# Two transformer blocks on one core: seven block products instead of eight in the feed-forward, expert strips loaded in pairs, unused products on TensorE

## What is computed

```python
def expert_choice_ffn(h, w_router, w_gate, w_up, w_down):   # 16 experts, 32 tokens each
    aff = softmax(h @ w_router)
    gates, idx = lax.top_k(aff.transpose(0, 2, 1), cap)
    xe = h[bidx, idx]
    a = einsum('becd,edf->becf', xe, w_gate)                # 1024 -> 2048
    b = einsum('becd,edf->becf', xe, w_up)
    ye = einsum('becf,efd->becd', silu(a) * b, w_down)      # 2048 -> 1024
    return zeros_like(h).at[bidx, idx].add(ye * gates)
...
x = x + g * rms_norm(p @ w_ple_proj, norm_ple_post)         # first block's end, "first projection"
...
kv = rmsnorm(mem, g_mem) @ w_mem_kv                         # second block's memory keys and values
...
h = rmsnorm(x, g_pre_ffn)                                   # second block's feed-forward
gate, up = split(h @ w_ffn_in)                              # 1024 -> 2 x 2816
x = x + rmsnorm((silu(gate) * up) @ w_ffn_down, g_post_ffn) # 2816 -> 1024
```

## Time and profile before

| | |
|---|---|
| median of 3 runs | 1776.91 us (1776.56 to 1779.11) |
| the profiled execution | 1774.88 us, its span 1773.1 us |
| TensorE busy | 1419.3 us, 80% |
| weight loads (beside it) | 769.1 us |
| VectorE, ScalarE, GpSimd busy | 324.1, 187.7, 34.6 us |
| DMA | 517.66 MB, mean 292 GB/s |
| granted clock | 0.91 |

### The profile page before, as it was taken

The page is one execution under the profiler, slowest core; times in us unless marked ns, Lnnn a source line. Parts: engine busy times, 40 slices in busy tenths (PEclk is TensorE's granted clock), DMA queues, the critical chain, the costliest instruction groups (busy, mean ns, idle before and its releaser), DMA issues.

```text
span 1773.1 us, 19596 instructions
## 1 busy us (share of the span) xinstructions
PE 1419.3 (80%) x7856; PEld 769.1 (43%) x7856; DVE 324.1 (18%) x798; ACT 187.7 (11%) x509; POOL 34.6 (2%) x96
## 2 busy tenths in 40 slices
PE   8978656766666567666666679999999999999998
PEld 5533111211121112111211126878777888677775
DVE  2442001200110011011001112345334101200001
ACT  2221000000000000000000001133223000100000
POOL 1100000000000000000000000000000000000000
PEclk9999888887887888878888879999999999999999
DMA  9668999999999999999999992123130336034431
GB/s 402 242 250 354 427 427 431 426 428 428 428 428 427 428 429 426 428 428 428 429 427 429 427 429 103 64 107 109 50 157 24 152 144 262 35 123 172 173 148 48
DMA packets 41112, 517.66 MB, mean 292 GB/s; under 512 B 4592, under 2 KB 5616, under 8 KB 8048
## 3 DMA queue, kind: packets, MB, share of 16 engines
q1 hardware_dynamic: 39152, 513.98, 69.4%
q10 hardware_dynamic: 1920, 3.11, 0.5%
HBM read 515.50 MB, written 1.05 MB: 291 GB/s over the span
## 4 chain that ended last, share of the span: by engine, by line
PE 53%; DMA 42%; DVE 2%; issue 1%; ACT 1%; SPq 0%; POOL 0%; ACTq 0%; POOLq 0%; PEldq 0%; DVEq 0%
PE ps L898 51%; DMA ring<-in_experts 42%; PE ps L1263 1%; PE ps L904 1%; DVE turned_T L1511 1%; ACT xn L770 0%; DVE scr L1623 0%; DMA vecs<-in_vecs 0%; PE ps L981 0%; ACT scr L776 0%; DVE xn L1747 0%; PE ps L957 0%; SPq L180 0%; PE ps L1357 0%; DVE scr L1591 0%
## 5 line engine op out<-in xcount | busy, mean ns | idle before, releaser
L898 PE MATMUL ps<-ring,scr 128*32 128x512 f32 (+1 forms) x3200 | 549.4, 744 | 260.7 <-DMA ring<-in_experts 245.5
L898 PEld LDWEIGHTS ps<-ring,scr 128*32 128x32 f32 (+1 forms) x3200 | 130.3, 128 | 638.8 <-DMA ring<-in_experts 400.3
L898 PE MATMUL ps<-turned_T,ring 128*128 128x256 f32 (+2 forms) x1984 | 384.4, 363 | 7.3 <-PE ps L898 3.1
L898 PEld LDWEIGHTS ps<-turned_T,ring 128*128 128x128 f32 (+1 forms) x1984 | 334.5, 186 | 57.9 <-issue 14.7
L898 PE MATMUL ps<-scr 128*128 128x512 f32 (+10 forms) x640 | 158.8, 406 | 19.5 <-DVE scr L1623 13.0
L898 PE MATMUL ps<-ring,turned_T 128*128 128x128 f32 (+3 forms) x640 | 170.8, 425 | 2.3 <-DVE turned_T L1511 1.5
L898 PEld LDWEIGHTS ps<-ring,turned_T 128*128 128x128 f32 x640 | 106.3, 190 | 64.4 <-issue 49.0
L898 PEld LDWEIGHTS ps<-scr 64*128 64x128 f32 (+4 forms) x640 | 83.2, 173 | 95.5 <-issue 51.4
L1626 DVE TENSOR_TENSOR x<-x,ps 128x512 f32<-128x512 f32 x64 | 44.0, 687 | 261.2 <-PE ps L898 261.2
L1618 DVE SCALAR_TENSOR_TENSOR scr<-scr,ps 128x512 f32<-128x512 f32 x16 | 11.0, 688 | 279.5 <-PE ps L898 279.5
L1616 DVE SCALAR_TENSOR_TENSOR scr<-scr,ps 128x512 f32<-128x512 f32 x16 | 11.0, 688 | 198.9 <-ACT scr L691 198.9
(11 more groups left out here) (243 smaller groups left out, 631.1 us busy)
## 6 DMA issues: line engine op xcount, KB each, us to landing
ring<-in_experts SPq DMA_DIRECT2D x188, 2048.0 KB, 24.6
ring<-in_w_ffn_in SPq DMA_DIRECT2D x11, 2048.0 KB, 9.1
ring<-in_w_merge SPq DMA_DIRECT2D x8, 1536.0 KB, 6.4
ring<-in_w_ffn_down SPq DMA_DIRECT2D x11, 1024.0 KB, 4.8
ring<-in_w_out SPq DMA_DIRECT2D x4, 2048.0 KB, 23.7
ring<-in_w_ml SPq DMA_DIRECT2D x4, 2048.0 KB, 7.8
ring<-in_w_nsa SPq DMA_DIRECT2D x4, 2048.0 KB, 7.7
ring<-in_w_proj SPq DMA_DIRECT2D x8, 1024.0 KB, 6.1
```

Of the source, the lines that this page charges most:

```text
L898: return pe.matmul(o, l, rr, start=start, stop=stop)
```

## The change

1. **Feed-forward.** Rows, columns and tokens are each cut in two, and seven products of blocks take the place of eight: sums of weight blocks, token blocks and results are made by VectorE. `ff_in` does it for each strip from step 1 on (step 0 stays), with 7 x 8 matmuls of 128 columns; step s's weight sums (`sums_in`) are made in step s-2. All 11 inputs' steps now come first, `hF` holds their results, and then `ff_down` pairs row block n with n + 11: seven matmuls of 512 columns for each of 11 strips, in seven banks. At the end VectorE puts the seven banks together (`total`) before ScalarE's squares and `post(1, 1.0)`. VectorE's `post` uses one buffer, now in `gains`.
2. **Expert strips.** From expert 2 on the first ten strips of an expert are loaded two at a time, 32 KB a partition in one DMA into two neighbouring slots (`load_two`), once both are free; the last two come singly. All groups use the same slots (`ROT`).
3. **First projection and memory weights.** They go to slot 9, no longer into the ring; the projection is issued after four strips of expert 1 and after expert 0's `h_sb`, each memory quarter after the first expert of its group.
4. **Products without use.** `idle` multiplies constants into bank 7: 6 products of 256 columns at the start, and 5, 22 and 4 of 128 columns in the router.

```diff
+HALF = D_FF // P // 2
+FF_SLOTS = [2, 4, 3, 5]
...
-ROTS = [3, 4, 5, 0]
-LAST_ROT = 1
-TAIL = [(n + LAST_ROT - 3) % SLOTS for n in range(SLOTS)]
+ROT = 2
+PAIRED = {0: (2, 2), 1: (2, 1), 2: (2, 2), 3: (2, 0), 4: (2, 2), 5: (2, 0)}
+TAIL = [(n + ROT - 3) % SLOTS for n in range(SLOTS)]
...
+    def load_two(self, slot, dst, src):
+        for s in (slot, slot + 1):
+            r = self.rounds[s]
+            self.eng.wait_ge(self.free[s], r)
+            if not isinstance(r, int):
+                self.eng.nop(nofuse=True)
+        self.eng.dma_start(dst, src).then_inc(self.full[slot], 16)
+        self.count(slot, 1)
+        self.count(slot + 1, 0)
...
-                    r.load(s, whole(s, "experts", e * 12 + n))
-            def experts(part, rot):
-                with sp.Fori(0, PARTS[part]) as i:
-                    r.enter(i, {s: (2, 2) for s in range(SLOTS)})
-                    expert(i + sum(PARTS[:part]), around(rot))
-                    r.leave(PARTS[part])
+                    r.load(s, strip_of(s, e, n))
+            def paired(e, slots):
+                for n in range(0, 10, 2):
+                    s = slots[n]
+                    r.load_two(s, ring[:, s * SLOT:(s + 2) * SLOT], packed["experts"][bass.ds((e * 6 + n // 2) * P, P), :])
+                for n in (10, 11):
+                    r.load(slots[n], strip_of(slots[n], e, n))
+            def experts(part, rot, first=0):
+                n = PARTS[part] - first
+                with sp.Fori(0, n) as i:
+                    r.enter(i, PAIRED)
+                    paired(i + sum(PARTS[:part]) + first, around(rot))
+                    r.leave(n)
+            def with_aside(part, quarter):
+                if quarter:
+                    paired(sum(PARTS[:part]), around(ROT))
+                    sp.wait_ge(mkv_ps, quarter)
+                else:
+                    for n, s in enumerate(around(ROT)):
+                        if n == 4:
+                            sp.wait_ge(h_sb, 1)
+                            sp.dma_start(*whole(9, "w_ple_proj", 0)).then_inc(full[9], 16)
+                        r.load(s, strip_of(s, 1, n))
+                    sp.wait_ge(e_ps, 4)
+                sp.dma_start(*whole(9, "w_mem_kv", quarter)).then_inc(full[9], 16)
+                experts(part, ROT, 1)
 
             expert(0, FIRST_SLOTS, FIRST_LOADS)
-            r.load(2, whole(2, "w_ple_proj", 0))
             for n in range(4):
-                experts(1 + n, ROTS[n])
-                r.load(ROTS[n], whole(ROTS[n], "w_mem_kv", n))
-            experts(5, LAST_ROT)
+                with_aside(1 + n, n)
+            experts(5, ROT)
...
+            for s in range(FF_STEPS):
+                r.load(FF_SLOTS[s % 4], whole(FF_SLOTS[s % 4], "w_ffn_in", s, tslot))
+            for n in range(HALF):
+                s = FF_SLOTS[(FF_STEPS + n) % 4]
+                r.load(s, whole(s, "w_ffn_down", n, tslot))
...
+            def idle(n, a):
+                for _ in range(n):
+                    mm(bank[7][:, 0:a.shape[1]], a[:, 0:P], a)
+            pe.wait_ge(idle_in, 1)
+            idle(6, sA[:, 0, 0, :])
...
+            idle(5, ident)
             pe.wait_ge(route_sb, 3)
...
+            idle(22, ident)
...
+                def arrived(s, n):
+                    if single or n % 2 == 0 or n == 11:
+                        r.arrived(s, 1)
+                    else:
+                        r.count(s, 0)
...
+            idle(4, ident)
             pe.wait_ge(sel_done, 2)
             pe.wait_ge(xn_done, 4)
-            expert(0, FIRST_SLOTS, selall[:, 0])
+            expert(0, FIRST_SLOTS, selall[:, 0], True)
...
-            r.arrived(2, 1)
-            wple = slot[2][:, 0:2 * D].rearrange("p (k n) -> p k n", k=2)
+            pe.wait_ge(full[9], 32)
+            wple = slot[9][:, 0:2 * D].rearrange("p (k n) -> p k n", k=2)
...
+            def ff_in(s, at):
+                par, b = at % 2, hT.rearrange("p (j k) (t n) -> p j t k n", j=2, t=NT)
+                w = tstrip[FF_SLOTS[at]].rearrange("p (j k) (i n) -> p j i k n", j=2, i=2)
+                sums = sF[1 - par]
+                half = lambda q: bank[4 - 4 * par + q // 2][:, (q % 2) * T:(q % 2 + 1) * T]
+                r.arrived(FF_SLOTS[at], 1)
+                if not isinstance(s, int) or s > 1:
+                    pe.wait_ge(ff_h, s * 2 - 2)
+                    pe.nop(nofuse=True)
+                for q, (l, rr) in enumerate(((w[:, 0, 0], b[:, 0, 0]), (w[:, 1, 0], b[:, 1, 0]),
+                                             (sums[:, 1], tT[:, 1]), (sums[:, 0], tT[:, 0]), (sums[:, 3], b[:, 1, 1]),
+                                             (sums[:, 2], tT[:, 2]), (w[:, 1, 1], tT[:, 3]))):
+                    if q == 2:
+                        pe.wait_ge(ff_sum, s + 1)
+                        pe.nop(nofuse=True)
+                    for f in range(2):
+                        for k in range(4):
+                            ins = mm(half(q)[:, f * P:(f + 1) * P], l[:, k, f * P:(f + 1) * P], rr[:, k, :], k == 0, k == 3)
+                            if (q, f, k) == (0, 0, 0):
+                                ins.then_inc(tfree[FF_SLOTS[(at - 1) % 4]], 1)
+                    if q in (1, 3, 5, 6):
+                        ins.then_inc(ff_ps, 1)
...
+            def ff_down(n):
+                s = FF_SLOTS[(FF_STEPS + n) % 4]
+                w = tslot[s][:, 0:2 * D].rearrange("p (j i n) -> p j i n", j=2, i=2)
+                a = [[hF[:, c // 2, t, c % 2, :] for c in (n, n + HALF)] for t in range(NT)]
...
+                for q, (l, rr) in enumerate(((a[0][0], w[:, 0, 0]), (a[0][1], w[:, 1, 0]), (ss[:, 1], tt[:, 1]),
+                                             (ss[:, 0], tt[:, 0]), (ss[:, 3], w[:, 1, 1]), (ss[:, 2], tt[:, 2]),
+                                             (a[1][1], tt[:, 3]))):
...
+                    ins = mm(bank[q], l, rr, n == 0, n == HALF - 1)
...
+            with pe.Fori(0, 2) as i:
+                r.enter(i, {s: (1, 1) for s in FF_SLOTS})
+                for n in range(2, 6):
+                    ff_in(i * 4 + n, n % 4)
+                r.leave(2)
+            ff_in(10, 2)
+            for n in range(HALF):
...
+            dve.memset(sA[:, 0, 0, :], 1.0).then_inc(idle_in, 1)
...
+            def sums_in(s, at):
+                par = at % 2
+                w = tstrip[FF_SLOTS[at]].rearrange("p (j k) (i n) -> p j i k n", j=2, i=2)
+                o = sF[1 - par]
+                dve.wait_ge(tfull[FF_SLOTS[at]], (s - at) * 4 + 16 + landed[FF_SLOTS[at]])
+                dve.nop(nofuse=True)
+                chain(dve.tensor_tensor(o[:, 0], w[:, 0, 1], w[:, 1, 1], ALU.add))
+                sub(o[:, 1], o[:, 0], w[:, 0, 0])
+                sub(o[:, 2], w[:, 0, 0], w[:, 0, 1])
+                dve.tensor_tensor(o[:, 3], w[:, 1, 0], o[:, 1], ALU.subtract).then_inc(ff_sum, 1)
+            def sums_down(n):
...
+                if n > 2:
+                    dve.wait_ge(ffo_ps, n - 2)
+                dve.wait_ge(tfull[s], landed[s] + 16 * ((FF_STEPS + n) // 4 + 1))
+                chain(dve.tensor_tensor(ss[:, 0], a[1][0], a[1][1], ALU.add))
...
+                dve.tensor_tensor(tt[:, 3], w[:, 1, 0], tt[:, 1], ALU.subtract).then_inc(ff_sum, 1)
...
+            sums_in(1, 1)
...
+            def ff_in(s, par, h):
+                half = lambda q: bank[4 - 4 * par + q // 2][:, (q % 2) * T:(q % 2 + 1) * T].rearrange("p (f n) -> p f n", f=2)
+                dve.wait_ge(ff_ps, s * 4 - 1)
+                chain(dve.tensor_copy(u3F, half(0)))
+                total(gF[:, 0], half(1), u3F)
+                dve.wait_ge(ff_ps, s * 4)
+                total(u2F, half(2), u3F)
+                total(u3F, half(3), u2F)
+                dve.wait_ge(ff_ps, s * 4 + 1)
+                total(gF[:, 1], half(4), u3F, ff_h)
+                total(u2F, half(5), u2F)
+                total(uF[:, 1], half(3), u2F)
+                dve.wait_ge(ff_ps, s * 4 + 2)
+                total(uF[:, 0], half(6), u2F)
+                if h is not None:
+                    h()
+                dve.wait_ge(ff_th, s + 2)
+                chain(dve.scalar_tensor_tensor(out=gF, in0=thF, scalar=1.0, in1=gF, op0=ALU.add, op1=ALU.mult))
...
+                dve.scalar_tensor_tensor(out=dst, in0=gF, scalar=0.5, in1=uF, op0=ALU.mult, op1=ALU.mult).then_inc(ff_h, 1)
+            with dve.Fori(0, 2) as i:
+                chain.enter(i, 4 * (7 + 3 + 1))
+                for n in range(1, 5):
+                    ff_in(i * 4 + n, n % 2, lambda: sums_in(i * 4 + n + 2, (n + 2) % 4))
+                chain.leave(2)
+            sums_down(0)
+            ff_in(9, 1, None)
+            sums_down(1)
+            ff_in(10, 0, None)
+            for n in range(2, HALF):
+                sums_down(n)
+            dve.wait_ge(ffo_ps, HALF)
+            chain(dve.tensor_copy(v3F, bank[0]))
+            total(yF[:, 0, 0, :], bank[1], v3F, ff_h)
...
+            dve.wait_ge(ffo_ps, HALF + 1)
```

(11 more changed lines are left out.)

203 lines of the change are left out of this document (102 added, 101 removed).

## The result

The changed kernel takes 1757.19 us, the median of 4 runs (1754.44 to 1760.48), against 1776.74 us (1776.26 to 1779.11, 4 runs) of the kernel before beside it: a ratio of 0.9888, interval 0.9867 to 0.9909. That is 19.6 us less; 1756.5 was predicted, faster by over 0.2%. The profiled execution took 1758.83 us with a span of 1757.0, only 16.1 us less than the span before. In all rows a count is one of passes, two to a float32 product; the recorded expectations call some of these passes products.

A forecast was written before the change was run, and what follows sets the result against it. Expert stage bound by DMA bytes (428 GB/s), feed-forward by TensorE's products; -13.2 - 0.3 - 9.5 + 3.7 - 4 + 5 - 0.8 - 0.3 = -19.4 us gave 1756.5 us, range 1746 to 1768.

The forecast's parts named there:

- Feed-forward products: Feed-forward on TensorE: input products -13.2 us, one wait on its own last product -0.3, output products -9.5.
- VectorE under cover: Feed-forward steps: VectorE's sums, 10.5 us under TensorE's 12.5, cost nothing, with 2 us to spare per step.
- The end: After the last product: six sums delay VectorE's post-normalization, last write 8.6 us after TensorE instead of 4.9, +3.7 us.
- Pairs: Expert stage: loading strips two at a time doubles the rows and halves packets and completion marks, -4 us.
- a further doubling saves at most that: Expert strip rows: 8 to 16 KB saved 0.6%, so doubling again saves at most that, 4 us.
- Rival 2: Expert stage: long rows carry more than the small step, 1748 to 1752 us; chance 0.12.
- First projection: Near 170 us: weights land later, at 177, TensorE waits some 9 us, seventh strip is delayed; +5 us, bounds +3 to +8.
- Rival 1: First projection: its weights come in time, or the stream does not run dry, 1751.5 us; chance 0.12.
- Idle products: Start and router: idle products raise the clock, first projection starts 0.5 us earlier without gaps, -0.8; router waits filled, -0.3.
- The sum: Whole kernel: all terms together -19.4 us, 1755.5 or 1757.5 by starting value, taken as 1756.5; chance 0.52.
- rivals 3 and 4: 3: pairs or idle products give nothing, 1761 to 1765 us, chance 0.10; 4: VectorE sets feed-forward pace, 1766.5 us, 0.06.
- 5: Expert stage: stream runs dry once per expert, shown by slices under 420; 1798 us with 3 us each; chance 0.05.

The follow-up runs named there:

- proj_early: The changed kernel with the first projection's weights issued behind two strips of expert 1 instead of four: 1753.1 us.
- kc_late: keep_clock with the first projection's weights back behind four strips of expert 1: 1750.6 us.
- kc_single: keep_clock with all expert strips loaded singly instead of in pairs: 1749.4 us.
- keep_clock: proj_early plus idle products at five more places after the expert stage where TensorE waits: 1744.3 us.
- kc_old_ff: keep_clock with the feed-forward of the kernel before: 1764.0 us.
- kc_no_start: keep_clock without the change's idle products at the start and in the router: 1748.6 us.
- pairs_16k: The changed kernel with each strip pair still one DMA but kept apart in DRAM, giving two 16 KB rows per partition: 1765.7 us.
- vector_plus_2: The changed kernel with two more VectorE operations of 1024 elements in each of ten feed-forward input steps: 1761.1 us.

## Why the prediction was right, and where it was not

1. **Feed-forward products** (-13.2, -0.3, -9.5 = -23.0): 22.9 measured. The step that carried it was to count passes by the duration of their own shape, 112 x 0.1116, and not by columns; 12.51 and 6.01 us came out.
2. **VectorE under cover** (0): right. I had 10.5 us of work and 2 to spare per step; the two runs with added work give 10.2 and 2.3. What I did not have is that the lead of a step hides some more.
3. **The end** (+3.7): +3.0. The cause that I gave was only half right. The last quarter is complete at 1749.02, 2.4 us after TensorE (2.7 predicted), and VectorE begins the post-normalization at 1748.93; but the root that it needs is ready only then too (ScalarE's square of the second quarter, then two operations of GpSimd, to 1748.90), so the totals of the other half cost nothing extra there. I also wrote that before, the first half was over before TensorE ended; it ended 1.2 us after (1766.94 against 1765.71).
4. **Pairs** (-4): -5.2. The step that failed is "a further doubling saves at most that": I took the gain from 8 to 16 KB rows, 0.6%, as its upper bound, from a stretch of 2.5 us, and 16 to 32 KB gave 0.65% over 800 us. The bound itself was read too low: by packet, 8 KB rows cost 313 ns, so that doubling saved 12 ns of 626, 1.9%, and the next one 10 of 1228, 0.8%. It is the row and not the DMA. The Trainium skill (DMA: Bandwidth & Descriptors, Specifications) has a fabric ceiling of 435 GB/s; the trace goes from 428 to 431, still under it. Rival 2 (8 to 12 us) took the whole of that gap and falls. The Trainium skill (DMA: Bandwidth & Descriptors, Anatomy of one DMA — SWDGE (gpsimd) path) gives the 2.0 us per DMA for DMAs that GpSimd issues; the prediction puts it in another section there. Here, where SyncE issues them into a full queue, they are nowhere to be seen: with 67 double DMAs in place of 134 single ones, and rows of the same length, the queue moved 342.19 MB against 342.12.
5. **First projection** (+5): landing 177.19 (177 predicted), wait 8.93 (9), expert 1's first product 189.65 (187.7 to 191.1), seventh strip 198.88 (197.3 to 202.1). It cost 5.2 to 6.3 us by proj_early's trace and 5.0 by kc_late's. Rival 1 falls.
6. **Idle products** (-0.8 and -0.3): 0.47 at the start, since the six hold the transposes until 6.46, 0.4 later than before; these then take 2.26 us instead of 3.68. In the router 0.1: the five run at 1.2 GHz, 2.48 us instead of the 1.1 that I gave them, and VectorE's selections end as before. What I left out is that without them the input projection and expert 0 ran at half clock for a while in two of four traces, 4.3 to 4.6 us in all; before's profiled execution did not show that case, and I did not look for it.
7. **The sum**: 1757.2 against 1756.5, and this is closer than its terms. Up to the gate product -0.1 was predicted and +0.3 measured, but the pairs gave 1 to 2 us more than I said, the late weights cost up to 1.3 more, and the idle products gave half of their term. The 1756.5 lies between two sums that start from two values of the kernel before, 2 us apart. The rivals 3 and 4 did not come. Nor did 5: the slices under 420 that I named as its sign occur, but 430 to 432 GB/s in each window of 200 us leave no room for a dry queue in every expert.

What I left out altogether is the middle, where the same instructions take 441.5 to 451.3 us. It made the profiled spans differ by 16.1 us, and whoever reads terms from two whole spans would have put 3.5 us in the wrong place; it also blurred the medians. Why the clock falls at one of these places in one execution and at another in the next stays open: kc_late and kc_single lost it inside the 128 narrow passes with the same unused products as keep_clock, kc_old_ff and kc_no_start, which kept it. Unused products ahead of those narrow ones were not tried.

## What to carry to other kernels

Count a changed product by the time of its own shape at the granted clock, and price a moved load by what it does to the next slot that comes free, not by the wait that it makes (here 8.9 us of wait, 5 to 6 us of time). Before splitting a difference of two profiles into terms, compare both spans stage by stage, those that the change does not touch first; here this gave the feed-forward to 0.1 us where medians wander by several. Where such a stage wanders, try a few unused products in the waits ahead of where the clock falls (here 9 us in the median, 3.5 in the lowest time). A cover is known only when it has been filled: add work to the hidden engine until it shows, and compare the two engines' periods, as a lead can hide an engine that is already the slower one.

## What the hardware did that I had not expected

- From 1060 to 1540 us TensorE is busy for 460 of 480 us, and still it falls to 1.2 GHz for some microseconds, in some executions of a program and not in others: behind waits of 0.9 to 1.7 us, and in five traces (proj_early, pairs_16k, vector_plus_2, kc_late, kc_single) inside the 128 narrow passes, 2.4 to 2.6 us after they had begun, with a wait of 0.74 us ahead of them. With three to six unused products in the waits the granted clock of the middle was 1.00 throughout in three traces of five.
- Rows of 32 KB carry 0.65% more than rows of 16 KB in a full queue (344.56 against 342.34 MB in 800 us); two 16 KB rows in one DMA carry what two DMAs carry. Rows of 8, 16 and 32 KB take 313, 614 and 1218 ns.
- After six unused products from 1.18 us on, the 16 transposes at 6.46 take 2.26 us; they took 3.68 at half clock before. With them the input projection ran at 2.4 GHz in all but one of ten traces, without them in two of four; expert 0's first 96 passes did in eight of ten with the unused products and in two of four without.
